# Adding the first layer's expert rows inside the second layer's input projection

## The reference

```python
p_l = ada_norm(x, g_mix[i], sh1, sc1) @ w_in[i]
p_c = ada_norm(xc, g_mix[i], csh1, csc1) @ w_in[i]
...
y = hier_moe(tokens, r_w_group[i], r_b_group[i], r_w_expert[i], r_b_expert[i], e_w1[i], e_w3[i], e_w2[i])
x = x + ga2 * y[:bsz * n_lat].reshape(bsz, n_lat, d)
if update_ctx:
    xc = xc + cga2 * y[bsz * n_lat:].reshape(bsz, n_ctx, d)
```

## Time and profile before

| what | us |
|---|---|
| median of three runs | 4847.15 |
| lowest and highest | 4845.9 and 4850.27 |
| the profiled execution | 4848.02 |
| its span | 4846.0 |
| TensorE busy in it | 4058.8 (84%) |
| VectorE busy in it | 2163.2 (45%) |

### The profile page before, as it was taken

How to read it: one execution, slowest core, us unless ns; L and a number is a source line. 1 busy time by engine, 2 the same in 40 slices (tenths; PEclk the granted TensorE clock), 3 DMA queues, 4 the chain that set the end, 5 groups by cost and what they waited for, 6 DMA issues and landing times. The chain is left out here.

```text
span 4846.0 us, 90034 instructions
## 1 busy us (share of the span) xinstructions
PE 4058.8 (84%) x38594; PEld 2401.3 (50%) x38594; DVE 2163.2 (45%) x2888; ACT 1195.2 (25%) x1971; POOL 509.7 (11%) x522
## 2 busy tenths in 40 slices
PE   4998979979999796999938988799689988688893
PEld 1443545658888453443414444366578874333341
DVE  1465437755666543111133654377566656310014
ACT  0221127742322110101001211177332322100001
POOL 0232310001000100000021323200000000000001
PEclk7999968989999897999968999799899999799996
DMA  8467441024332755998976665500323214499996
GB/s 339 129 174 202 134 120 29 23 65 128 103 106 78 277 232 234 402 405 355 396 293 206 171 205 156 131 24 23 98 58 90 65 49 175 198 385 388 390 428 237
DMA packets 252294, 932.77 MB, mean 192 GB/s; under 512 B 37076, under 2 KB 100500, under 8 KB 223264
## 3 DMA queue, kind: packets, MB, share of 16 engines
q1 hardware_dynamic: 205752, 756.31, 42.2%
q0 software_dynamic: 28704, 117.20, 8.4%
q10 hardware_dynamic: 17480, 53.95, 2.8%
HBM read 722.31 MB, written 165.77 MB: 183 GB/s over the span
## 5 line engine op out<-in xcount | busy, mean ns | idle before, releaser
L806 PE MATMUL ps<-w,hT 128*128 128x480 f32 (+3 forms) x2240 | 885.9, 555 | 1.4 <-ACT hT L611 1.4
L2644 PE MATMUL ps<-w,xT 128*32 128x512 f32 (+2 forms) x3104 | 669.1, 612 | 68.3 <-DMA w<-in_e_w 59.7
L806 PEld LDWEIGHTS ps<-w,hT 128*128 128x128 f32 x2240 | 435.5, 198 | 430.7 <-issue 407.8
L2587 DVE TENSOR_TENSOR sg<-sg,ps 128x512 f32<-128x512 f32 x46 | 31.6, 687 | 975.3 <-ACT sg L2375 975.3
L2644 PEld LDWEIGHTS ps<-w,xT 128*32 128x32 f32 (+2 forms) x3104 | 239.1, 137 | 459.7 <-issue 447.0
L1118 DVE TENSOR_REDUCE nm<-ps 128x1 f32<-128x1280 f32 (+1 forms) x216 | 295.8, 1370 | 145.7 <-PE ps L1209 145.7
L1209 PE MATMUL ps<-KT,qs 32*128 32x512 f32 (+3 forms) x1200 | 288.8, 600 | 50.5 <-DMA ident<-in_k_ident 24.4
L2644 PE MATMUL ps<-w,hT 128*32 128x512 f32 (+2 forms) x1552 | 324.9, 594 | 3.5 <-ACT hT L2366 3.5
L1076 ACT ACTIVATE work<-ps,nm 128x1280 f32<-128x1280 f32 (+1 forms) x216 | 265.9, 1231 | 97.2 <-DVE nm L1118 93.1
L2120 PE MATMUL ps<-w_out,yT 128*128 128x512 f32 x576 | 256.7, 604 | 14.6 <-ACT yT L1960 14.6
L594 ACT ACTIVATE po<-ps 128x480 f32<-128x480 f32 (+3 forms) x140 | 75.2, 539 | 657.2 <-PE ps L806 648.9
(11 more groups left out here) (326 smaller groups left out, 5318.4 us busy)
## 6 DMA issues: line engine op xcount, KB each, us to landing
w<-in_e_w SPq DMA_DIRECT2D x192, 2048.0 KB, 20.2
wt<-in_w_mod SPq DMA_DIRECT2D x8, 3072.0 KB, 25.1
w_mod<-in_w_mod POOLq DMA_DIRECT2D x3, 8192.0 KB, 31.2
s_ye<-yo ACTq DMA_DIRECT2D x46, 512.0 KB, 10.8
w<-in_w_in SPq DMA_DIRECT2D x12, 1920.0 KB, 14.3
ra<-s_scan SPq DMA_DIRECT2D x160, 128.0 KB, 2.8
kb<-s_scan SPq DMA_DIRECT2D x160, 128.0 KB, 2.9
x<-s_x SPq DMA_DIRECT2D x36, 512.0 KB, 6.9
```

Source lines behind the costliest of these rows:

```text
L806: mm = pe.matmul(ps[:, c, a - c0:b - c0], hT[i % 2][:, t, :], w[:, c, t, a - c0:b - c0], start=(t == 0), stop=(t == DT - 1))
L2644: mm = pe.matmul(ps[lo:hi, bank, :], xs[:, t, lo:hi], w[p % 3][:, t, cols], start=(t == 0), stop=(t == nt - 1), skip_group_check=len(tiles ...
```

## The change

The combine stage is left out for layer 0. Its work moves into the input projection of layer 1, under the name `FUSE`:

- POOL gathers tile t's two expert rows to `ya` and `yb`, one buffer each, when tile t-1's sum is done (`gather`).
- VectorE does the same four passes (`add_experts`), the last of them into `x` in place; for tile i+2 they stand at the end of step i.
- ACT squares `x` only behind that sum, and then issues the store of `x` to memory, which the combine stage made before. SP loads the next tile's `x` only when this store has landed (`x_st`).
- `G` and `S` lose their second half, in both layers: the latents' `G`, `S` (and in layer 1 `GA`) are loaded over the context's when the norm of tile 1 is done, and `set_gain(0)` stands in step 1, ahead of the norm of tile 2.

```diff
@@ buffers @@
-        G, S = sb("G", [P, 2, D]), sb("S", [P, 2, D])
+        FUSE = layer > 0
+        G, S = sb("G", [P, D]), sb("S", [P, D])
+        if FUSE:
+            GA, ya, yb = sb("GA", [P, D]), sb("ya", [P, D]), sb("yb", [P, D])
@@ SP @@
                 def load_x(t):
                     if t > 0:
                         sp.wait_ge(x_used, t)
+                        if FUSE:
+                            sp.wait_ge(x_st, 16 * t)
...
+                    if FUSE:
+                        at = net.mod[layer - 1][j][5 * D:6 * D]
+                        sp.dma_start(GA[:], at.partition_broadcast(P)).then_inc(ga_in, 16)
+                    sp.dma_start(G[:], m[D:2 * D].partition_broadcast(P)).then_inc(g_in[j], 16)
+                    sp.dma_start(S[:], m[0:D].partition_broadcast(P)).then_inc(g_in[j], 16)
...
+                    if i == 0:
+                        sp.wait_ge(h_done, CT)
+                        load_mod(0)
                     if i == -1:
-                        load_mod(0)
@@ POOL @@
+                def gather(t):
+                    if t > 0:
+                        pool.wait_ge(x_sum, t)
+                    for j, y in enumerate((ya, yb)):
+                        pool.indirect_dma_start(y[:], None, net.ye,
+                                                bass.IndirectOffsetOnAxis(net.row[:, t, j:j + 1], 0)
+                                                ).then_inc(y_in, 16)
+
+                if FUSE:
+                    gather(0)
...
                 def step(i):
+                    if FUSE and i + 2 < NT:
+                        gather(i + 2)
@@ ACT @@
-                        act.wait_ge(x_in, 16 * (i + 2))
+                        if FUSE:
+                            act.wait_ge(x_sum, i + 2)
+                        else:
+                            act.wait_ge(x_in, 16 * (i + 2))
                         act.activation(h[:], x[:], ACT.Square, accum_out=small[:, 0:1]).then_inc(sq_done, 1)
+                        if FUSE:
+                            act.dma_start(rows(net.x, (i + 1) * P), x[:]).then_inc(x_st, 16)
@@ VectorE @@
+                def add_experts(t):
+                    gate = [net.gate[:, t, j:j + 1] for j in range(2)]
+                    dve.wait_ge(y_in, 32 * (t + 1))
+                    dve.tensor_scalar(ya[:], ya[:], gate[0], None, ALU.mult)
+                    dve.drain()
+                    dve.scalar_tensor_tensor(ya[:], yb[:], gate[1], ya[:], ALU.mult, ALU.add)
+                    dve.drain()
+                    if t in (0, CT):
+                        dve.wait_ge(ga_in, 16 if t < CT else 32)
+                    dve.tensor_tensor(ya[:], ya[:], GA[:], ALU.mult)
+                    dve.drain()
+                    dve.wait_ge(x_in, 16 * (t + 1))
+                    dve.tensor_tensor(x[:], x[:], ya[:], ALU.add).then_inc(x_sum, 1)
...
+                    if i == CT - 1:
+                        set_gain(0)
                     if i + 1 < NT:
                         norm_row(i)
-                    if i == 0:
-                        set_gain(0)
...
+                    if FUSE and i + 2 < NT:
+                        add_experts(i + 2)
@@ run_phases @@
-            stage(nc, net, ps, layer)
+            if stage is not combine_phase or layer == DEPTH - 1:
+                stage(nc, net, ps, layer)
```

More of the change, by code:

```diff
@@ L289, in input_projection_phase @@
         w = sb("w", [P, len(C_CHUNKS), DT, CHUNK])
-        G, S = sb("G", [P, 2, D]), sb("S", [P, 2, D])
+        FUSE = layer > 0
+        G, S = sb("G", [P, D]), sb("S", [P, D])
+        if FUSE:
+            GA, ya, yb = sb("GA", [P, D]), sb("ya", [P, D]), sb("yb", [P, D])
+        ga_in, y_in, x_sum, x_st = (sem(n) for n in ("ga_in", "y_in", "x_sum", "x_st"))
         x, h = sb("x", [P, D]), sb("h", [P, D])
@@ L311, in input_projection_phase @@
             "p (j w) -> p j w", j=2) for b in range(2)]
-        turned = G[:].rearrange("p j d -> p (j d)")[:, 0:QK_W]
+        turned = G[:, 0:QK_W]
         square = sq[:, 0:A_Q + A_KV]
@@ L378, in load_mod @@
                     m = net.mod[layer][j]
-                    sp.dma_start(G[:, j, :], m[D:2 * D].partition_broadcast(P)).then_inc(g_in[j], 16)
-                    sp.dma_start(S[:, j, :], m[0:D].partition_broadcast(P)).then_inc(g_in[j], 16)
+                    if FUSE:
[3 more added lines that the diff above has]
+                    sp.dma_start(S[:], m[0:D].partition_broadcast(P)).then_inc(g_in[j], 16)
                 def load_w(src, c, at, n):
@@ L501, in _ @@
                     sp.wait_ge(qk_st[b], 16 * (NT // 2))
+                if FUSE:
+                    sp.wait_ge(x_st, 16 * NT)
                 sp.wait_ge(outs_st, 64 * NT)
@@ L635, in step @@
                     if a is not None:
+                        if FUSE and a == 0:
+                            act.wait_ge(x_st, 16 * NT)
                         if a >= 2:
@@ L650, in set_gain @@
                     dve.wait_ge(g_in[j], 16 * (2 + j))
-                    dve.scalar_tensor_tensor(G[:, j, :], G[:, j, :], 1.0, gain, ALU.add, ALU.mult
+                    dve.scalar_tensor_tensor(G[:], G[:], 1.0, gain, ALU.add, ALU.mult
                                              ).then_inc(gains_set, 1)
                     dve.drain()
+                def add_experts(t):
[11 more added lines that the diff above has]
+                    dve.tensor_tensor(x[:], x[:], ya[:], ALU.add).then_inc(x_sum, 1)
+                if FUSE:
+                    add_experts(0)
                 set_gain(1)
@@ L666, in norm_row @@
                     t = i + 1
-                    m = 1 if t < CT else 0
                     dve.wait_ge(root_done, t + 1)
-                    dve.scalar_tensor_tensor(h[:], x[:], small[:, 3:4], G[:, m, :], ALU.mult, ALU.mult
+                    dve.scalar_tensor_tensor(h[:], x[:], small[:, 3:4], G[:], ALU.mult, ALU.mult
                                              ).then_inc(x_used, 1)
                     dve.drain()
-                    dve.tensor_tensor(h[:], h[:], S[:, m, :], ALU.add).then_inc(h_done, 1)
+                    dve.tensor_tensor(h[:], h[:], S[:], ALU.add).then_inc(h_done, 1)
                 def mix(j, part, done):
```

## The result

| | us |
|---|---|
| kernel before, median (4 runs) | 4846.52 (4841.57 to 4850.27) |
| changed kernel, median (4 runs) | 4812.22 (4803.23 to 4815.49) |
| ratio, 95% interval | 0.9924 (0.991 to 0.9939) |
| profiled execution of the changed kernel, its span | 4813.5, 4811.6 |

The change saves 34 us. The timeline of the changed kernel shows the head of the projection where the combine stage stood; it answers to the earlier trace rows. Columns as there: start, duration, engine, line, operation, and how long the engine was idle and for what.

What follows compares the result with a forecast made beforehand. Transfers bound the head, then each round's chain from the load of x through POOL's root and adding DMAs to the mix. Head gain 53.1 less round loss 20.5 gives 32.6 us: 4815.4 profiled, 4814.6 median; range 4803 to 4839.

Steps and rivals of the forecast that it cites:

- Turn of tile 1: Projection head: TensorE reaches tile 1 at 2520.3, 53.1 us earlier; ends 56 and 48.4 us.
- The single buffers at nothing: Head: reloading the latents' GA, G and S after tile 1's norm costs nothing, with 3 us of cover left.
- First to second mix: Layer 1's first interval between neighbour mixes, 32.07 us before: 2.9 us longer.
- (a): Each round: VectorE's last pass and its semaphore stand between x's arrival and ACT's square, 1.4 us.
- (b): Each round: two gather issues on POOL stand ahead of the root and adding DMAs, 1.4 us.
- (c): Each round: bytes of gathers and store move in front of the adding DMAs, 1.0 us; bounds 0 and 4.3.
- (d): Each round: the load of x waits for the last tile's store, issued 25 us before; costs nothing.
- 1 (adding DMAs starved): Rounds: (b) and (c) at their bad ends in all rounds; gain 6 to 13 us, 4834 to 4841; chance 0.18.
- Rival 2: POOL's queue: adding DMAs move only after gathers land, 11 us more six times; 14 us slower, 4861; chance 0.06.
- Rival 3: Head: gathers or the latents' modulation stand behind the weights, 15 us more; gain 18, 4830; chance 0.07.
- Rival 4: Rounds hide (b) and (c), only (a) stays; gain 45 to 48 us, 4801; chance 0.07.
- The second rule set beside the forecast: Rounds: by SBUF port contention, each second gather pays under VectorE's directions pass; (b) 2.8, sum about 26 us.

Runs made afterwards that it cites:

- Experiment 1: Kernel before with layer 0's combine stage left out and nothing in its place: 4788.7 us, ratio 0.9878.
- experiment 2: Changed kernel with expert rows gathered for tile 0 alone, all passes, stores and waits kept: 4799.9 us, ratio 0.9897.
- 3: Changed kernel with the gathers of tiles 1 to 9 cut to 64 bytes a row: 4807.6 us, ratio 0.9917.
- experiment 4: Changed kernel with POOL's adding DMAs moved ahead of the root and the gathers last, in both layers: 4760.5 us, ratio 0.9813.
- 5: Changed kernel with each round's two gathers issued directly behind the adding DMAs instead of ahead of the root: 4808.9 us, ratio 0.9911.
- 9: Changed kernel with the gathers of tiles 1 on fetching 16 rows of 4 KB instead of 128: 4803.2 us, ratio 0.9908.
- 11: Repeat of experiment 4, the changed kernel with the adding DMAs moved ahead of the root: 4766.3 us, ratio 0.983.
- experiment 12: Changed kernel with tile 0's gathers alone and four POOL buffer fills in place of each later tile's gathers: 4805.7 us, ratio 0.9907.
- experiment 7: Changed kernel with two buffers for x, so each tile's load goes out a step earlier: 4780.1 us, ratio 0.9857.

## Why the prediction was right, and where it was not

The prediction said 4814.6; the kernel takes 4812.2. What goes, what comes on top and where it stands in the way were read rightly. That the two figures lie 2.4 us apart is partly luck. The two parts were each a little off, in opposite ways: the head gave 1.9 us less, the rounds cost 2.6 us less. In the head one link was missing, in the round one term had the wrong cause. And the 7.65 us by which this execution came to the stage earlier are nearly made up by the 6.5 us that it took longer behind the rounds; the prediction had neither.

- **The part removed**, 62.0. Experiment 1 has 60.5 for it.
- **First product**, 0.9 late. The first pass came as foreseen (12.19 us behind the start, 11.9 foreseen). From the end of the sum to the product it took 9.21 us, not 8.62: POOL began its issues 0.8 us behind the sum.
- **Turn of tile 1**, 51.2 earlier, not 53.1. The step that failed is what the load of tile 1 waits for. The prediction named tile 0's norm and the landing of tile 0's store to `s_x`. That store left 1 us earlier than foreseen, at 16.97, and yet the load went out 2.2 us later than foreseen, at 28.39. In SP's order `store_hT` stands ahead of the load, and it waits for ACT's copies of tile 0's turned rows (done at 2494.77). It was issued from 2494.79 to 2496.96, and the load followed 0.11 us behind. In experiments 2 to 5, 9, 11 and 12 the load follows `store_hT` by the same 0.10 or 0.11 us, whether that store's issue took 0.34 us or 3.58. In the kernel before and in experiment 1, where no store to `s_x` has to land first, it follows by 0.04 and 0.05. So the landing never held it. How long it took no row tells, only that it was over in 8.05 us in experiment 2. The prediction's load, at 26.17, stood 0.9 us behind its own first product (25.27), which left no room for an issue of 2.17. No run moved this load ahead of `store_hT` alone; experiment 7 did so with a second buffer. (By its own terms the good end of this turn is 2516.8, not 2517.3.) The DMA engines were full all this time (first window up to the first product, second up to this turn; columns as in the earlier trace rows):

```profile
2468.60:2494.80 26.20, 1.94 (x8) 1.57 (x8) 8.29 (x8) 2.34 (x4) 5.59 (x8) 0.50 0.97 365
2494.80:2514.60 19.80, 8.59 (x17) 3.92 (x17) 7.15 (x7) 1.58 (x3) 2.51 (x3) 0.67 1.04 415
```

The load itself took 10.48 us, the 10.5 of the sum, and from arrival to turn 7.04, where the sum has 7.26. Why the issue of `store_hT` takes 0.34 us in some runs and 3.73 in others is not shown.

- **The single buffers at nothing.** Right, but only just. VectorE waited 7.01 us for the latents' `GA`, which was there at 2528.11, their gain pass at 2532.94 had no wait, and tile 2's norm ended just as TensorE came to its turn:

```profile
2524.59 12.62 PE L855 MATMUL ps<-w,hT 128*128 128x480 f32 x32
...
2528.11 1.23 DVE L696 TENSOR_TENSOR ya<-ya,GA 128x1024 f32<-128x1024 f32 x1 [7.01 <-DMA GA<-s_mod]
...
2532.94 1.22 DVE L683 SCALAR_TENSOR_TENSOR G<-G,pre 128x1024 f32<-128x1024 f32 x1
...
2535.99 1.23 DVE L719 TENSOR_TENSOR h<-h,S 128x1024 f32<-128x1024 f32 x1
...
2537.27 1.10 PE L868 MATMUL ps<-ident,h 128*128 128x128 f32 x8
```

The norm ends at 2537.22 and TensorE's products at 2537.21: nothing was lost. I had said that 3 us of cover were left; there were none. Experiment 7 shows the price behind it.

- **The first mix.** From tile 1's turn to it 49.76 us, before 48.18: 1.6 for the 1.0 of the sum.
- **First to second mix.** 0.9 in place of 2.9, the largest term by share that was mis-sized. The sum came at 2581.20, but ACT's square began 18.82 us behind the mix, as it had before (18.8): ACT had its own copies to make until then (its last one, of `gb`, began at 2582.68). I had let this hide 0.9 us of (a); it hid all of (a), and of the gathers all but 0.5 us at the root and 0.3 of landing.
- **A full round.** (a) the last pass, 1.4 foreseen, 1.2 by experiment 2. (b) the two issues, 1.4 foreseen: root 1.4 us later behind the sum (2.91 against 1.50), adding DMAs 1.3. (c) 1.0 foreseen, 0.6 measured (11.6 against 11.0), and for another reason: not the gathers' bytes (3) nor their rows (9), but the delay itself (12); that its size came near is luck, and what makes a late adding DMA slower stays open. (d) nothing, right: the wait for the store never showed. The sum was 3.8, the rounds took 38.3 - 34.9 = 3.4 us more, four times 13.6 for 15.2.
- **The last round** has no gather, 1.85 for 1.4.

Of the rivals, 1 (adding DMAs starved) did not come: the landing is 0.7 us longer than before, not the 4.3 of its bad end. Rival 2 (one after the other) is refuted by the rounds. The second gather landed 6.5 us behind its issue there (median), at 2743.3 in the round shown. Adding DMAs that began only then would have let the mix start at 2754.2; it started at 2750.39. Rival 3 came in a small way, 1.9 us for 15. Rival 4 was wrong: (b) and (c) are 2.2 us a round.

Whether the rule of the Trainium skill that the prediction set beside rivals 1 and 2 ("DMA: Bandwidth & Descriptors", Queues, rings and completion order) holds here, no run shows. Gathers of 4 KB rows, of 64-byte rows, of 16 rows and none at all give landings of 11.6, 12.0, 12.0 and 11.7 us behind the same delay, but even the largest had landed some 7 us ahead of the mix, so none was left to wait for.

The second rule set beside the forecast, a sum of 26, was priced wrongly. The 2.8 us for (b) are two long issues, where the sentence makes only the second one long; that gives 0.95 + 0.92 = 1.9 and a sum of about 31. And the second issue took 1.19 us, not 1.86: VectorE's pass under which it began was 0.69 us long, not 1.23. The contention itself is there (below).

What the prediction did not look for was the weak link itself. It wrote the chain down, saw POOL's root ahead of the adding DMAs, and priced what was added to it. That the link could be cut by a change of order, 42 us with the stage and some 50 without it, stood in the same rows.

## What to carry to other kernels

Where a stage's work is moved into a loop, follow the loop's round link by link first, and price each added instruction at the place where it stands in front of a link; here only one pass, two issues and the slower landing behind them counted, 3.4 us a round, and three passes and all bytes were free. If a DMA that is ready stands on its engine behind an instruction that waits for younger data, put the DMA first: that was worth as much as the fusion. And for each load ask not only what it waits for by name but what stands ahead of it on its queue: tile 1's load was held by a store that the prediction had left out. A single buffer that costs nothing has used up a cover; when the part ahead of it gets faster, it is the next wait.

## What the runs showed of the hardware

The length of a gather's issue went with what VectorE did, hardly with its size. 16 rows of 4 KB, 128 rows of 64 bytes and 128 rows of 4 KB took 0.99 + 1.21, 1.11 + 1.19 and 1.10 + 1.19 us. In experiment 4, where the gathers meet the mix:

```profile
2673.43 1.21 POOL L526 DMA_INDIRECT ya<-s_ye,row  x1 [0.17 <-issue]
...
2674.86 1.75 DVE L724 SCALAR_TENSOR_TENSOR pf<-pf,po 128x1536 f32<-128x1536 f32 x1
2674.95 2.52 POOL L526 DMA_INDIRECT yb<-s_ye,row  x1 [0.30 <-issue]
```

An issue that begins 0.09 us behind a two-input pass of 1.75 us takes 2.52 us. That agrees with the Trainium skill ("SBUF — State Buffer", Who interferes with whom), by which a VectorE instruction with two inputs in SBUF contends with a GpSimd one that reads SBUF (the gather's list of rows lies there). The pass ends at 2676.61, the issue 0.86 us later. In the kernel before, the issue of 1.86 us at 2490.60 began 0.17 us behind this pass and ended 0.80 us behind its end:

```profile
2490.43 1.23 DVE L2786 TENSOR_TENSOR mix<-mix,GA 128x1024 f32<-128x1024 f32 x1
```

In the round of the changed kernel the second issue (2736.80) began 0.35 us behind a pass of 0.69 us and ended 0.85 us behind its end. So in all three places the issue took what was left of the pass that had begun before it, and 0.80 to 0.86 us more, about one undisturbed issue. Passes that VectorE began later, during the issue, added nothing.

The other thing not expected: a delay of 1.3 us of the adding DMAs brought up to 1 us of longer landing in three rounds of four, with no byte added (experiment 12).
